# Attention by pairs of heads on the halves of the array, mask and maximum folded into one instruction, modulation columns by transposes

## What is computed

```python
s = jnp.where(mask[None, :, None, None], s, -jnp.inf)
m = jnp.max(s, axis=-1, keepdims=True)
if sink is not None:
    m = jnp.maximum(m, sk)
p = jnp.exp(s - m)
l = jnp.sum(p, axis=-1, keepdims=True)
if sink is not None:
    l = l + jnp.exp(sk - m)
o = jnp.einsum('bngrqk,bnkgd->bnqgrd', (p / l).astype(v.dtype), vv)
...
mod = silu_c @ w_mod[l] + b_mod[l]
mod_c = silu_cc @ w_mod[l] + b_mod[l]
sh1, sc1, g1, sh2, sc2, g2 = jnp.split(mod[:, None, :], 6, axis=-1)
```

## Time and profile before

| | |
|---|---|
| runs (us) | 2329.57, 2333.0, 2335.85 |
| median | 2333.0 |
| profiled execution | 2331.13 (its span 2329.4) |
| TensorE matmul busy | 2156.4 us, 93% |
| VectorE busy | 1169.1 us, 50% |
| ScalarE busy | 880.3 us, 38% |
| GpSimd busy | 179.0 us, 8% |
| mean granted TensorE clock | 0.953 of full speed |
| chain that ended last | TensorE 76%, VectorE 10%, DMA 6%, ScalarE 5% |

### The profile page before, as it was taken

One profiled execution on the slowest core, in us unless ns is written; L12 is line 12 of the kernel. 1 busy time (PEld: TensorE's weight loads), 2 busy tenths in 40 slices (PEclk: granted clock), 3 DMA queues, 4 the chain that ended last, 5 costly groups with the idle time before them and its releaser, 6 DMA issues.

```text
span 2329.4 us, 34518 instructions
## 1 busy us (share of the span) xinstructions
PE 2156.4 (93%) x14872; PEld 1885.9 (81%) x14872; DVE 1169.1 (50%) x1575; ACT 880.3 (38%) x1221; POOL 179.0 (8%) x165
## 2 busy tenths in 40 slices
PE   5889899999997999699989989999999799989998
PEld 5757799999687999578668877777787686988998
DVE  4464554465645555632553445444444525556554
ACT  4344543344444433422432233222222424444442
POOL 0021000002200000300350000000000002000000
PEclk8889999999999999789999999999999898999999
DMA  5256457865443455522033332544444320464553
GB/s 173 84 181 211 133 152 206 208 184 163 163 145 109 155 189 172 136 79 62 20 71 91 106 101 85 172 148 159 147 161 145 115 77 23 136 181 130 179 181 109
DMA packets 326934, 317.11 MB, mean 136 GB/s; under 512 B 12901, under 2 KB 311660, under 8 KB 326526
## 3 DMA queue, kind: packets, MB, share of 16 engines
q1 hardware_dynamic: 318976, 293.89, 40.9%
q0 software_dynamic: 3904, 12.03, 2.4%
q10 hardware_dynamic: 3902, 8.98, 1.1%
HBM read 306.02 MB, written 8.85 MB: 135 GB/s over the span
## 4 chain that ended last, share of the span: by engine, by line
PE 76%; DVE 10%; DMA 6%; ACT 5%; issue 2%; POOL 1%; SPq 0%; ACTq 0%; DVEq 0%; POOLq 0%
PE acc L575 20%; PE acc L576 19%; PE acc L577 19%; DVE w_low L1520 4%; ACT w_high L1119 3%; PE pso L759 3%; PE pss L734 2%; PE pst L748 2%; PE acc L590 2%; PE acc L591 1%; PE acc L592 1%; POOL scores L1047 1%; PE acc L660 1%; DVE normed L1536 1%; PE pst L697 1%
## 5 line engine op out<-in xcount | busy, mean ns | idle before, releaser
L1520 DVE TENSOR_TENSOR w_low<-raw,w_high 128x2048 fp32r<-128x2048 f32 (+3 forms) x252 | 545.5, 2165 | 486.8 <-ACT w_high L1119 486.2
L575 PE MATMUL acc<-normed,w_high 128*128 128x256 f32 (+2 forms) x2080 | 665.2, 320 | 17.1 <-DVE w_low L1520 16.2
L576 PE MATMUL acc<-normed,w_high 128*128 128x256 f32 (+2 forms) x2080 | 657.2, 316 | 0.0
L577 PE MATMUL acc<-normed,w_low 128*128 128x256 f32 (+2 forms) x2080 | 656.8, 316 | 0.0
L1119 ACT ACTIVATE w_high<-raw 128x2048 fp32r<-128x2048 f32 (+3 forms) x252 | 447.2, 1775 | 404.0 <-PE acc L577 300.8
L575 PEld LDWEIGHTS acc<-normed,w_high 128*128 128x128 f32 (+1 forms) x2080 | 400.9, 193 | 51.6 <-DVE w_low L1520 21.7
L577 PEld LDWEIGHTS acc<-normed,w_low 128*128 128x128 f32 (+1 forms) x2080 | 401.0, 193 | 23.8
L576 PEld LDWEIGHTS acc<-normed,w_high 128*128 128x128 f32 (+1 forms) x2080 | 401.0, 193 | 23.2
L575 PE MATMUL acc<-inner,w_high 128*128 128x256 f32 (+2 forms) x1160 | 367.0, 316 | 9.0 <-DVE w_low L1520 4.9
L576 PE MATMUL acc<-inner,w_high 128*128 128x256 f32 (+2 forms) x1160 | 364.3, 314 | 0.0
L577 PE MATMUL acc<-inner,w_low 128*128 128x256 f32 (+2 forms) x1160 | 363.8, 314 | 0.0
(11 more groups left out here) (173 smaller groups left out, 2326.0 us busy)
## 6 DMA issues: line engine op xcount, KB each, us to landing
raw<-in_w_ff SPq DMA_DIRECT2D x64, 1024.0 KB, 5.4
raw<-in_w_mod SPq DMA_DIRECT2D x48, 1024.0 KB, 5.1
raw<-in_w_in SPq DMA_DIRECT2D x48, 512.0 KB, 3.9
raw<-in_l_w_gate SPq DMA_DIRECT2D x22, 1024.0 KB, 5.4
raw<-in_l_w_up SPq DMA_DIRECT2D x22, 1024.0 KB, 5.6
raw<-in_w_in SPq DMA_DIRECT2D x18, 1024.0 KB, 5.4
raw<-in_l_w_down SPq DMA_DIRECT2D x16, 1024.0 KB, 5.5
raw<-in_l_w_qkv SPq DMA_DIRECT2D x12, 1024.0 KB, 5.1
```

The costliest lines, as they stand in the source:

```text
L575: mm(dst, lh, rh, start=i == 0, stop=False)
L576: mm(dst, lh, rl, start=False, stop=False)
L577: ins = mm(dst, ll, rh, start=False, stop=i == n - 1)
L1520: V.tensor_tensor(WL[:, s % NSPLIT, 0:nw], RAW[:, slot_of[u], 0:nw], WH[:, s % NSPLIT, 0:nw].bitcast(F32), ALU.subtract).then_inc(w_low, 1)
```

## The change

1. **Pairs.** The loops of all engines run over pairs of tasks. TensorE computes the scores of both tasks in turns (first task, second task, first, second), each into its own bank, and the two outputs likewise. Score slots and statistics grow from three to four. Neighbourhood tasks are reordered so that a pair is two heads at the same block of queries.
2. **Masked block.** With `past=True` the first query block has 128 keys instead of 256: 384 score columns, three transposes, a second output product of 128 columns; GpSimd's share is 128 columns.
3. **Fold.** One `tensor_tensor_reduce` per query block adds the mask to the scores, negates, and takes the minimum, which starts from the negated sink or from a large number. The scale moves into the ScalarE copies of the queries. Where there is no mask, `none` is an array of zeros. A neighbourhood task needs two folds, the second starting from the first one's result.
4. **Output.** ScalarE rounds straight from the output bank and VectorE writes the low part from it. A second output bank (`spare`) takes turns with `pso`.
5. **Modulation.** 8 of the 16 units of the first mixer move into the first neighbourhood attention; each attention with units takes one in each of its first 8 pairs. `columns` uses four transposes into a full bank, and VectorE sums four groups of rows (`tensor_reduce`) before the bias. The gains of the second norm are computed behind the neighbourhood attention, and the merges behind it wait earlier for its stored outputs.

```diff
-        SM = sb("scores", [P, 3, BANK])
+        SM = sb("scores", [P, 4, BANK])
...
-            modulation(DIL_LOTS * MODS if l else SWA_LOTS * MODS)
+            modulation(MODS)
...
+            if l == 0:
+                modulation(MODS)
             for b, (name, kt) in enumerate(BR):
...
+            masks = [none, none] if mask is None else [mask[:, 0:P] if past else mask[:, 0:S], mask[:, S:2 * S]]
+            rows = [(0, 0, P if past else S, masks[0]), (1, S, S, masks[1])]
+            if past:
+                turns = [(0, 0), (S, P), (S + P, S)]
+                sums = [(v[0], 0, S, 0), (v[1], S, P, P)]
+            else:
+                turns = [(0, 0), (P, S), (S, P), (S + P, S + P)]
+                sums = [(v[0], 0, S, 0), (v[1], S, S, 0)]
...
+            tasks = [one_block(2 * i + e, b) for i in range(NA_H // 2) for b in range(NB) for e in range(2)]
...
                 for c in range(4):
-                    ins = mm(cols_bank[p][:, 2 * c:2 * c + 2], RSTD[:, P * c:P * c + P], const("sel"),
-                             start=True, stop=True)
+                    ins = nc.tensor.transpose(cols_bank[p][:, P * c:P * c + P], RSTD[:, P * c:P * c + P], ident)
```

TensorE's attention:

```diff
+                def scores(j):
+                    i = first + 2 * j
+                    if i:
+                        pe.wait_ge(max_done, i)
+                    for n in range(2):
+                        for e in range(2):
+                            q, k, at = tasks[2 * j + e]["scores"][n]
+                            ins = mm(PSS[e][:, at:at + k.shape[1]], q, k, start=True, stop=True)
+                            if n:
+                                ins.then_inc(s_full, 1)
...
+                def output(j):
+                    pe.wait_ge(t_copied, first + 2 * j + 2)
+                    last = max(lots[2 * j], lots[2 * j + 1])
+                    if last >= 2:
+                        need(stores + last - 1)
...
+                scores(0)
+                for j in range(pairs + 2):
+                    if j + 1 < pairs:
+                        scores(j + 1)
+                    if 0 < j <= pairs:
+                        turn(2 * j - 2)
+                    if mods and j == mods + 1:
+                        all_columns()
+                    if j > 1:
+                        output(j - 2)
+                    if j < mods:
+                        modulate((rows, rows), cols)
+                    if 0 < j <= pairs:
+                        turn(2 * j - 1)
```

ScalarE's and VectorE's attention:

```diff
+                def probs(n):
+                    i = first + n
+                    act.wait_ge(t_full, i + 1)
+                    if i >= 2:
+                        act.wait_ge(o_full, i - 1)
...
+                def output(n):
+                    d = tasks[n]["dst"]
+                    if d is not None:
+                        act.wait_ge(o_full, first + n + 1)
...
+                for j in range(pairs + 3):
+                    if mods:
+                        modulation_rows(rows + min(j, mods) // 2)
+                    for e in range(2):
+                        if j < pairs:
+                            exps(2 * j + e)
+                        if 0 < j <= pairs:
+                            probs(2 * j - 2 + e)
+                    for e in range(2):
+                        if j > 2:
+                            output(2 * j - 6 + e)
...
+                def fold(n, row, low, to):
+
+                    i = first + n
+                    q, c, w, mask = tasks[n]["rows"][row]
+                    return V.tensor_tensor_reduce(SM[:, i % 4, c:c + w], PSS[i % 2][:, c:c + w], mask, -1.0, low,
+                                                  ALU.add, ALU.min, STAT[:, i % 4, to:to + 1])
+
+                def maxima(j):
+                    a, i = 2 * j, first + 2 * j
+                    dve.wait_ge(s_full, i + 2)
+                    if i >= 4:
+                        dve.wait_ge(t_full, i - 2)
...
+                def output(n):
+                    d = tasks[n]["dst"]
+                    if d is not None:
+                        dve.wait_ge(high_done, st["store"] + 1)
+                        st["store"] += 1
+                        V.tensor_tensor(d.low[:, 0, :], out_bank(first, lots[n])[:, 0:S],
+                                        d.high[:, 0, :].bitcast(F32), ALU.subtract).then_inc(stored, 1)
+
+                for j in range(pairs + 3):
+                    if j < pairs:
+                        maxima(j)
+                    for e in range(2):
+                        if 0 < j <= pairs:
+                            inverse(2 * j - 2 + e)
+                    if mods:
+                        modulation(done + (mods if j >= mods + 2 else min(j - 2, mods - 2)) // 2)
+                    for e in range(2):
+                        if j > 2:
+                            output(2 * j - 6 + e)
```

More of the change, by code:

```diff
@@ L427, in na_tasks, with lots_before, out_bank @@
             return tasks
+        def lots_before(tasks):
+            return [sum(t["dst"] is not None for t in tasks[:i]) for i in range(len(tasks) + 1)]
+        spare = {}
+        def out_bank(first, lot):
+            return spare[first] if lot % 2 else PSO
         first_in = sem("first_in")
@@ L716, in rotate, with attention @@
                     ins.then_inc(acc_full, 1)
-            def attention(tasks, lots=0):
-                accs = [PSACC[(st["acc"] + 1 + i) % 4] for i in range(2)]
-                cols = PSACC[(st["acc"] + 3) % 4]
-                for g in range(st["acc"] - 4 if lots else st["acc"] - 1, st["acc"]):
+            def attention(tasks, mods=0):
+                first, pairs = st["task"], len(tasks) // 2
+                cols, rows, spare[first] = (PSACC[(st["acc"] + i) % 4] for i in (1, 2, 3))
+                for g in range(st["acc"] - 4, st["acc"]):
@@ L738, in turn @@
-                def turn(i):
-                    t = tasks[i - first]
+                lots, stores = lots_before(tasks), st["store"]
+                def scores(j):
[8 more added lines that the diff above has]
+                                ins.then_inc(s_full, 1)
@@ L766, in attention @@
-                scores(first)
-                scores(first + 1)
-                for i in range(first, last):
-                    if i + 2 < last:
-                        scores(i + 2)
-                    if lots and (i - first) % (len(tasks) // (lots * MODS)) == 0:
-                        modulate(accs, cols)
-                    turn(i)
-                    if i > first:
-                        output(i - 1)
-                output(last - 1)
-                st["task"] = last
+                    for at, to in tasks[n]["turns"]:
+                        ins = nc.tensor.transpose(PST[:, to:to + P], SM[:, i % 4, at:at + P], ident)
@@ L779, in by_tile @@
+                st["store"] += lots[-1]
+                st["task"] += len(tasks)
             def by_tile(T):
@@ L1233, in attention @@
-                    if i > first + 2:
-                        output(i - 3)
-                    st["task"] += 1
-                probs(st["task"] - 1)
-                for j in range(max(first, st["task"] - 3), st["task"]):
-                    output(j)
+                def probs(n):
[3 more added lines that the diff above has]
+                        act.wait_ge(o_full, i - 1)
+                    w = P * len(tasks[n]["turns"])
+                    nc.scalar.activation(PT[:, i % 2, 0:w], PST[:, 0:w], ACT.Copy).then_inc(t_copied, 1)
@@ L1430, in _ @@
                     st["acc"] += i == 0
-                attention(na_tasks(l))
+                attention(na_tasks(l), 0 if l else MODS)
                 for b3 in range(3):
@@ L1494, in _ @@
             pending = []
+            BIG = 3.0e38
             def link(ins):
```

300 lines of the change are left out of this document (119 added, 181 removed).

## The result

| | before | changed |
|---|---|---|
| median (us) | 2332.6 (4 runs) | 2382.4 (4 runs, 2377.7 to 2390.9) |
| profiled execution's span | 2329.4 | 2377.7 |
| mean granted clock | 0.953 | 0.932 |

What follows compares the result with a forecast made beforehand. TensorE throughput bounds the kernel before; pairing nearly closes a loop through output copy, low half and folds. 2331.1 + 116 (attention stages, mixed clock) - 4.5 (column sums) = 2442 us, range 2350 to 2535.

Steps and rivals of the forecast that it cites:

- the side: Whole program: the change makes the kernel slower, chance 0.83, against 0.14 for faster and 0.03 for within 0.3%.
- the 4.5 itself: Column sums in the second block's feed-forward: transposes save 0.39 us in each of twelve groups, 4.5 us less.
- the price of the clock: Six attention stages: 488 us at 1.2 GHz, 325 at the high clock; the middle, 407, taken: +116 against before.
- the high-clock sum: Six attention stages with the clock high: 325 us against 290.4, 35 us more.
- The loop: One pair's closed loop at the high clock: dilated 7.4 us, low-rank 8.4, neighbourhood 8.2 or 7.8, cross-attention 10.9.
- the prediction's own test: VectorE in attention: the prediction is wrong if a fold with its reading takes other than 0.4 to 0.65 us.
- Entry and missing parts at the ends taken as equal: Six attention stages: each costed as pairs times loop, with nothing added for filling or running dry.
- (a): Rival, attention stages: the clock stays high, +35 - 4.5 gives 2361 us; chance 0.17.
- (b): Rival, attention stages: the clock stays low, +198 - 4.5 gives 2524 us; chance 0.17.
- (c): Rival, scores and outputs: pairs don't overlap where matmuls alternate halves, some 56 us more at high clock, 2526; chance 0.06.
- (d): Rival, attention stages: loop not closed, the busiest engine sets the pace, stages 210 us, program faster at 2246; chance 0.15.
- break-even of 7.4 us a pair: Attention stages: (290.4 + 4.5) / 40 pairs, the loop length deciding faster or slower; forecast high-clock loops average 8.1.

Runs made afterwards that it cites:

- both: Changed kernel with ScalarE's output copy moved between the two groups of exponentials and six score slots instead of four: 2281 us, ratio 0.973 to 0.981.

## Why the prediction was right and wrong

**Right:** the bound (a loop closed by way of output copy, low half and folds); the side; TensorE at 64% in the stages (60 forecast), a wait ended by the fold in each pair, 2.4 to 2.9 us where an output is stored (3 forecast) and 1.4 to 1.8 where none is, the granted clock 0.75 in the dilated stage (0.6 to 0.85), its loops with an output 8.3 to 9.0 us (7.4 to 11.4), score starts 0.1 us apart. Outside the stages 2.5 us less (4.5) is within what profiles differ by there; the 4.5 itself was 12 x 0.39 = 4.7, and 4.2 by the groups as measured. The bound was only half seen: the wait for one of four score slots closes the loop as well, nearly at the same moment, and the prediction did not have it.

**Wrong, the size.** The stages took 341 us, not 407: 66 less. The step that moved the sum most is the price of the clock, 82 us where filling the waits gave back 34, so 48 of the 66. The other 18 are the high-clock sum (325, and 307 measured with the waits filled), where two larger errors cancelled, one in the loop and one at the ends. By the steps of the forecast:

- *The loop.* A low-rank loop at the high clock measured 6.6 and 7.2 with columns, not 8.4. Four folds with their readings took 1.2 us, not 1.9 (the prediction's own test, 0.4 to 0.65 us a fold, fails: 0.21 and 0.34); low-rank scores 1.41, not 1.86; from the output copy to the first fold 0.76, not 0.92 (copy, handover and low half). I had added the fold's busy time and a reading, while the reading (0.08) lies under the end of the fold and the next instruction starts 0.07 earlier. And the loops that store nothing have neither copy nor low half: the two in the dilated stage took 4.7 and 5.3 us, below the 7.4 that the prediction gave as the least.
- *The ends.* "Entry and missing parts at the ends taken as equal" failed outright, though its error did not reach the sum. With the clock held up the stages took 307 us, near the 325 forecast for it, but made otherwise: 34 loops of 5.8 us and six ends of 18 us, where I had 40 loops of 8.1. Two errors of 60 to 80 us nearly cancelled, by luck.
- *The clock.* Granted as forecast, but priced too high: 34 us instead of 82. I doubled TensorE's whole part of a loop (+4.0 us dilated) and took half of it. In the trace mostly pieces of a loop are low: between 638.32 and 646.63 the first turn, the output and the columns run at the low clock, scores, modulation and second turn at the high one: 8.3 us. The loop before it, low in nearly all its pieces (granted clock 0.65), took 9.0, which is 2.7 more than the same loop with the waits filled (6.3, 615.31 to 621.63 in that run), where I had 7.4 + 4.0 = 11.4.

**The fold.** The Trainium skill (VectorE: DVE Perf Modes, the section on two Vector instructions with no wait between them) counts an accumulating instruction as two, and its rules for kernel authors would have one not fuse. The second instruction is in the trace, but it costs nothing that shows between starts, and undoing the fold cost 77 us; here the measurement decides for the fold. As a rule on time it would have put the undone kernel at no change.

**Rivals.** (a), the clock stays high, 2361: filling the waits gave 2339. (b) and (c) did not come: the clock fell in pieces, and a pair's eight score instructions took 0.85 us from start to start in the past-masked stages of "both". (d) was one slot pair and one moved copy away. Its break-even of 7.4 us a pair was passed by the loops alone, 6.3 us on average with the low clock in them (213 us in 34); with 21 us at each of the six ends the sum stayed positive all the same.

## What to carry to other kernels

When work is paired or batched to fill one engine, count the loops a stage needs to fill and to run dry, and multiply by the new, longer loop: here TensorE had 44 us less to do, and stood idle for 55 us more in the leads and 40 us more at the six ends. When an engine's program waits for something that was ready a loop ago, look for an unrelated instruction ahead of it in program order, and test each closing way alone and both together, since either one hides the other. Before a stage with waits is costed at one clock, look whether cheap filler would hold it there.

## What the hardware showed that I had not expected

- A fold with its accumulator reading takes 0.34 us from start to start over 256 columns and 0.21 over 128, as much as one plain instruction of that size (four such instructions, two of each width, 1.17 us in the undone kernel; four folds 1.10). The forms of the changed kernel, count, busy us and mean ns:

```profile
L1718 DVE CUSTOM_DVE_ANT_0 scores<-pss,silc 128x256 f32<-128x256 f32 x64 | 23.9, 420 | 57.0 <-PE pst L763 47.0 <-PE pss L752 10.0
L1718 DVE CUSTOM_DVE_ANT_0 scores<-pss,bias,stat 128x256 f32<-128x256 f32 x32 | 14.1, 479 | 0.0
L1718 DVE DVE_READ_ACCUMULATOR2_ANT stat<- 128x1 f32 x160 | 13.2, 83 | 0.0
```

  The fold that starts from another column's value (second row) takes 0.06 us more. (`silc` in the first row is the array of zeros, which lies in that buffer.)
- Products on two halves of the array overlap in full without alternating when each task has two of them (0.85 us for a pair's eight score instructions in either order), and lose half a microsecond when each has four (1.52 us for 1.03).
- Twelve transposes of the identity in each wait made the stages 34 us shorter, and the program 44 us faster.
